# Value half of the up-projection from seven half-size products instead of eight

## The chip, the core and the metric

The kernel runs on one core of a Trainium2 chip. The metric is device time in microseconds (us) of one execution; lower is better. The core has a matrix engine (TensorE, "PE" in the profile; its weight loads are shown apart as "PEld"), three engines for elementwise work (VectorE "DVE", ScalarE "ACT", GpSimd "POOL") and a queue engine (SyncE "SP") that here issues nearly all transfers. Each engine runs its own instructions strictly in the order in which they are written; engines wait for one another only on semaphores. TensorE reads its operands from SBUF and adds up in the eight banks of PSUM (128 partitions x 512 float32 each).

## The reference

Two layers over x of shape (1, 512, 1024). Layer 0 mixes tokens by a Mamba-2 scan, layer 1 by causal pooling; each is followed by a gated feed-forward block, and that block is what the change touches:

```
def conv_ffn(u, w_up, conv_w, conv_b, w_down):
    h = u @ w_up                                  # (512,1024) x (1024,5632)
    h = causal_depthwise_conv(h, conv_w, conv_b)  # width 3, over tokens
    gate, val = split(h, 2)                       # 2816 columns each
    return (silu(gate) * val) @ w_down            # (512,2816) x (2816,1024)
```

All is float32, between RMS norms.

## The kernel before, in words

A float32 product is made of three passes on TensorE. Each operand is split in a high part (a copy rounded to TensorE's fp32r format) and a low part (the rest, by a subtraction), and `three_passes` (L306) adds high x high, high x low, low x high.

Weights come in slabs of 1 MB (128 partitions x 2048 numbers): in the up-projection a slab is 256 columns, so two output blocks of 128 columns, and eight k-blocks. SP loads slab n to `raw[n % 2]` (`load`, L263), which may be overwritten once slab n-2 has been split. ACT makes `w_hi` (`split_hi`, L268), DVE makes `w_lo` (`split_lo`, L274). There are two pairs of `w_hi`/`w_lo`, so a split also waits until TensorE has done with the slab two before.

The up-projection of a layer has 22 slabs, in 11 iterations of the index i: a slab of gate columns, then one of value columns (`up_pe`, L1142). A slab is 2 blocks x 8 k-blocks x 3 passes = 48 matmuls of 512 tokens, an iteration 96. The four blocks of an iteration are numbered q = 0 to 3 (0, 1 gate; 2, 3 value) and go to banks 4 to 7; `tmp` has one slot for each. After block q ACT makes the first tap of the convolution with the bias (`last_tap`, L524; the profile shows L525), DVE adds the other two (`other_taps`, L527; L534, each a 128x511 and a 128x510 instruction). After the gate blocks ACT makes the silu (L1171). DVE multiplies gate and value (L1189), ACT and DVE split the result to `act_hi` and `act_lo` (L1174, L1193), which the down-projection reads as its stationary operand.

The order of all this is written out by hand, one program for each engine. In an iteration ACT (`up_act`, L1152) runs: first taps q0 q1, silu q0 q1, split of the value slab, first taps q2 q3, `act_hi` twice; the split of the gate slab comes first. DVE (`up_dve`, L1177) runs: `split_lo`, taps q0 q1, `split_lo`, taps q2 q3, two products, two `act_lo`. Iterations 2 to 10 are a loop on the engine. The down-projection follows with 11 slabs of 48 matmuls (`down_pe`, L1040 in the profile).

GpSimd builds constants at the start, adds squares in the mixer (L862, a 128x512 addition) and does nothing in the feed-forward blocks.

## Time and profile before

| | |
|---|---|
| median of 3 runs | 1138.78 us (1138.66 to 1138.9) |
| profiled execution | 1138.84 us, of which span 1137.1 us |
| TensorE busy | 99% of the span |
| DVE, ACT, POOL busy | 61%, 46%, 3% |
| matmuls | 5730 |
| moved by DMA | 121.74 MB, mean 107 GB/s |

The profiled execution is one execution recorded by the hardware; its span runs from its first to its last recorded instruction. "Busy" is the share of the span in which an engine works on an instruction. TensorE's matmuls overlap in the records, so the distance between the starts of two of them, not the duration of one, says what a matmul costs.

### The profile page before, as it was taken

The numbers are of one execution on the slowest core, as the hardware profiler recorded it, in microseconds if no ns is written. First come the engines' busy times: TensorE is split into PE (matmuls) and PEld (weight loads), VectorE is DVE, ScalarE is ACT, GpSimd is POOL, SyncE is SP. The second block draws the span as 40 slices with busy tenths as digits, with TensorE's granted clock in tenths as the row PEclk, the third lists the DMA queues.
The fourth block names the chain that finished last, engine by engine and source line by source line (L and its number), as shares of the span: only waits on it lengthen the run. The fifth ranks groups of instructions, "written<-read, shape, count | busy, mean of one in ns | idle before, by whom it ended". The sixth has DMA issues, their size and how long they took to land.

```text
span 1137.1 us, 14741 instructions
## 1 busy us (share of the span) xinstructions
PE 1127.7 (99%) x5730; PEld 949.7 (84%) x5730; DVE 695.5 (61%) x825; ACT 524.2 (46%) x610; POOL 35.9 (3%) x93
## 2 busy tenths in 40 slices
PE   8999999999999999999999999999999999999998
PEld 7888888888888988888888888899888888888886
DVE  6778889999763865655655321597655565552124
ACT  5667676767533643443443221475443434331213
POOL 6000000000100000000000000000000000000000
PEclk9999999999999999999999999999999999999999
DMA  8244343433233133233233223512232232323221
GB/s 274 76 133 148 121 128 122 133 127 130 75 111 126 61 111 111 79 106 111 74 111 108 98 90 111 167 38 75 93 111 94 91 109 76 110 85 115 96 74 74
DMA packets 85390, 121.74 MB, mean 107 GB/s; under 512 B 4215, under 2 KB 71391, under 8 KB 85344
## 3 DMA queue, kind: packets, MB, share of 16 engines
q1 hardware_dynamic: 85162, 121.02, 32.0%
q8 instruction: 33, 0.54, 0.2%
q14 instruction: 13, 0.11, 0.0%
q10 hardware_dynamic: 182, 0.07, 0.0%
HBM read 118.92 MB, written 2.16 MB: 106 GB/s over the span
## 4 chain that ended last, share of the span: by engine, by line
PE 99%; DMA 1%; ACT 0%; DVE 0%; issue 0%; SPq 0%; DVEq 0%
PE bank L1040 29%; PE bank L307 19%; PE bank L308 19%; PE bank L309 19%; PE bank L515 6%; PE bank L801 1%; PE bank L792 1%; PE bank L753 1%; PE bank L743 1%; PE bank L431 1%; PE bank L1214 1%; DMA raw<-in_ssd_w_in 1%; PE bank L1229 0%; PE bank L1230 0%; PE bank L1231 0%; PE bank L721 0%
## 5 line engine op out<-in xcount | busy, mean ns | idle before, releaser
L307 PE MATMUL bank<-h_hi,w_hi 128*128 128x512 f32 x928 | 364.5, 393 | 0.0
L309 PE MATMUL bank<-h_hi,w_lo 128*128 128x512 f32 x928 | 361.5, 390 | 0.0
L308 PE MATMUL bank<-h_lo,w_hi 128*128 128x512 f32 x928 | 361.2, 389 | 0.0
L277 DVE TENSOR_TENSOR w_lo<-raw,w_hi 128x2048 fp32r<-128x2048 f32 x90 | 206.1, 2289 | 215.0 <-ACT w_hi L272 215.0
L534 DVE SCALAR_TENSOR_TENSOR tmp<-bank,par,tmp 128x511 f32<-128x511 f32 (+2 forms) x248 | 184.9, 747 | 125.3 <-ACT tmp L525 112.4
L272 ACT ACTIVATE w_hi<-raw 128x2048 fp32r<-128x2048 f32 x90 | 171.7, 1908 | 154.0 <-PE bank L1040 152.3
L309 PEld LDWEIGHTS bank<-h_hi,w_lo 128*128 128x128 f32 x928 | 174.2, 188 | 37.1
L307 PEld LDWEIGHTS bank<-h_hi,w_hi 128*128 128x128 f32 x928 | 174.3, 188 | 36.2 <-issue 0.8
L308 PEld LDWEIGHTS bank<-h_lo,w_hi 128*128 128x128 f32 x928 | 174.4, 188 | 35.0
L525 ACT ACTIVATE tmp<-bank,par 128x512 f32<-128x512 f32 x112 | 86.2, 774 | 221.7 <-PE bank L309 201.4
L1040 PE MATMUL bank<-w_lo,act_hi 128*128 128x512 f32 x348 | 107.2, 389 | 0.0
L1040 PE MATMUL bank<-w_hi,act_lo 128*128 128x512 f32 x348 | 107.1, 389 | 0.0
L1040 PE MATMUL bank<-w_hi,act_hi 128*128 128x512 f32 x348 | 107.1, 389 | 0.0
L1040 PEld LDWEIGHTS bank<-w_hi,act_lo 128*128 128x128 f32 x348 | 65.3, 188 | 13.6
L1040 PEld LDWEIGHTS bank<-w_lo,act_hi 128*128 128x128 f32 x348 | 65.3, 188 | 13.5
L1040 PEld LDWEIGHTS bank<-w_hi,act_hi 128*128 128x128 f32 x348 | 65.3, 188 | 13.4
L1174 ACT ACTIVATE act_hi<-tmp 128x512 f32 (+1 forms) x44 | 27.3, 633 | 55.8 <-DVE tmp L1189 55.8
L1040 PE MATMUL bank<-w_hi,y_hi 128*128 128x512 f32 x128 | 40.1, 394 | 0.0
L1171 ACT ACTIVATE tmp<-tmp 128x512 f32<-128x512 f32 x44 | 27.6, 626 | 26.5 <-DVE tmp L534 26.4
L1040 PE MATMUL bank<-w_lo,y_hi 128*128 128x512 f32 x128 | 39.5, 390 | 0.0
L1040 PE MATMUL bank<-w_hi,y_lo 128*128 128x512 f32 x128 | 39.5, 389 | 0.0
L1193 DVE TENSOR_TENSOR act_lo<-tmp,act_hi 128x512 f32 (+1 forms) x44 | 28.7, 690 | 6.3 <-ACT act_hi L1174 5.9
(203 smaller groups left out, 1030.1 us busy)
## 6 DMA issues: line engine op xcount, KB each, us to landing
raw<-in_ffn_w_up SPq DMA_DIRECT2D x44, 1024.0 KB, 5.0
raw<-in_ffn_w_down SPq DMA_DIRECT2D x22, 1024.0 KB, 4.8
raw<-in_ssd_w_in SPq DMA_DIRECT2D x19, 1024.0 KB, 5.2
decay<-ac_dram SPq DMA_DIRECT2D x16, 512.0 KB, 5.5
raw<-in_ssd_w_out SPq DMA_DIRECT2D x8, 1024.0 KB, 4.8
from_start<-ac_dram SPq DMA_DIRECT2D x32, 128.0 KB, 4.6
xres<-in_x SPq DMA_DIRECT2D x4, 512.0 KB, 6.0
result<-xres SPq DMA_DIRECT2D x3, 512.0 KB, 2.6
```

What stands on the lines that cost most here:

```text
L272: act.activation(w_parts(n, i)[0][:], raw[n % 2][:], ACT.Copy).then_inc(hi_ready, 1)
L277: dve.tensor_tensor(lo[:], raw[n % 2][:], hi[:].bitcast(F32), ALU.subtract).then_inc(lo_ready, 1)
L307: pe.matmul(dst, wh, xh, start=first, stop=False, **kw)
L308: pe.matmul(dst, wh, xl, start=False, stop=False, **kw)
L309: return pe.matmul(dst, wl, xh, start=False, stop=last, **kw)
L515: mm = pe.matmul(bank[:, 2 * s + j, ts], w[:, k, j * P:(j + 1) * P], x[:, k, ts], start=turn == 0 and k == 0, stop=turn == 2 and k == DB - 1)
L525: act.activation(tmp[:, slot, :], bank[:, source, :], ACT.Identity, bias=b, scale=w).then_inc(conv_tap, 1)
L534: dve.scalar_tensor_tensor(tmp[:, slot, back:], bank[:, source, 0:T - back], w, tmp[:, slot, back:], ALU.mult, ALU.add).then_inc(conv_part ...
L1040: mm = pe.matmul(bank[:, 2 * c + j, :], x[:, cs(c)], w[:, k, j * T:(j + 1) * T], start=start, stop=stop)
L1171: act.activation(tmp[:, j, :], tmp[:, j, :], ACT.Silu).then_inc(gate_silu, 1)
L1174: act.activation(act_hi[:, bass.ds(2 * i + j, 1), :].rearrange("p a l -> p (a l)"), tmp[:, 2 + j, :], ACT.Copy).then_inc(act_hi_ready, 1)
L1193: dve.tensor_tensor(act_lo[:, blk, :].rearrange("p a l -> p (a l)"), tmp[:, 2 + j, :], act_hi[:, blk, :].rearrange("p a l -> p (a l)").bit ...
```

## The change: seven products for the value slabs

In iterations 2 to 10 of each layer (18 value slabs in all; `SEVEN0 = 2`) the value slab is no longer 48 matmuls of 512 tokens. Weights (2 column blocks x 2 halves of k) and features (2 halves of k x 2 halves of the tokens) are taken as 2 x 2 blocks, and their product is made of seven block products instead of eight (Winograd's form of Strassen's scheme). A block product is 4 k-blocks x 3 passes = 12 matmuls of 256 tokens, so a slab is 84 of these (`seven_pe`), in banks 0 to 3.

What that adds:

- POOL forms the sums of feature blocks once per layer (`combos_pool`, ten 128x1024 instructions), ACT and DVE split them to `t_hi`, `t_lo` (four 128x1024 instructions each).
- POOL forms the four sums of weight blocks for each value slab in place, in `raw` (`weights_pool`, four instructions of 4x128 = 512 numbers per partition), after that slab has been split; ACT and DVE split the result, in two halves of 128x1024 (`weights_hi_act`, `weights_lo_dve`), to the other pair of `w_hi`/`w_lo`. `raw` is free only after that.
- ACT keeps the first product (`first_seven_act`, 128x256), and four DVE instructions add the seven up to the two value blocks in the SBUF tile `val` (`sevens_dve`). The taps of q2 and q3 read `val`.

What moves: the taps of q2 and q3 of an iteration and the split of the next value slab change places (the taps are ahead) on ACT and DVE. The product gate x value is kept unsplit in `gated`; `act_hi`/`act_lo` are gone, and their part is made in the down phase, one 128x1024 instruction on ACT and DVE for each down slab (`down_hi_act`, `down_lo_dve`; that of slab 0 in iteration 4). The loops are written out in full instead of looped. The first down slab begins with its chunks 2 and 3.

On DVE, in one iteration before (the loop's body from the value slab's split on; the pair of L534 rows stands twice, for q2 and q3):

```order
L277 TENSOR_TENSOR w_lo<-raw,w_hi 128x2048 [waits hi_ready]
...
L534 SCALAR_TENSOR_TENSOR tmp<-bank,par,tmp 128x511
...
L534 SCALAR_TENSOR_TENSOR tmp<-bank,par,tmp 128x510
...
L1189 TENSOR_TENSOR tmp<-tmp 128x512 [waits conv_done,gate_silu]
...
L1193 TENSOR_TENSOR act_lo<-tmp,act_hi 128x512
```

And an iteration on DVE after the change, from the second tap of q0 on (number 3; L1287 is `weights_lo_dve`, L1301 to L1308 are `sevens_dve`, the first L312 splits the next gate slab and the second the next value slab, L1381 is gate x value):

```order
L569 SCALAR_TENSOR_TENSOR tmp<-bank,par,tmp 128x510 [waits conv_part]
L1287 TENSOR_TENSOR w_lo<-raw,w_hi 128x1024 [waits ws_hi_ready] x2
L569 SCALAR_TENSOR_TENSOR tmp<-bank,par,tmp 128x511 [waits conv_tap]
L569 SCALAR_TENSOR_TENSOR tmp<-bank,par,tmp 128x510 [waits conv_part]
L312 TENSOR_TENSOR w_lo<-raw,w_hi 128x2048 [waits hi_ready]
L1301 TENSOR_TENSOR val<-val,bank 128x2x256 [waits p_done,p1_kept]
L1304 TENSOR_TENSOR val<-val,bank 128x2x256 [waits blk_done,c_step]
L1306 TENSOR_TENSOR val<-val,bank 128x256 [waits c_step]
L1308 TENSOR_TENSOR val<-val,bank 128x2x256 [waits c_step]
L569 SCALAR_TENSOR_TENSOR tmp<-val,par,tmp 128x511 [waits conv_tap]
...
L312 TENSOR_TENSOR w_lo<-raw,w_hi 128x2048 [waits hi_ready]
L1381 TENSOR_TENSOR gated<-tmp 128x512 [waits conv_done,gate_silu] x2
```

The taps of q2 and q3 now stand between the seven products' sums and the value slab's split, and both splits of a slab's sums stand between the taps of q0 and q1.

On ACT, the same iteration after the change (L1281 is `weights_hi_act`, L1339 the silu, L1294 the kept product):

```order
L560 ACTIVATE tmp<-val,par 128x512 [waits u_ready,c_ready] x2
L307 ACTIVATE w_hi<-raw 128x2048 [waits blk_done,slab_in1]
L560 ACTIVATE tmp<-bank,par 128x512 [waits u_ready,blk_done]
L1339 ACTIVATE tmp<-tmp 128x512 [waits conv_done]
L1281 ACTIVATE w_hi<-raw 128x1024 [waits w_sum,blk_done]
L1281 ACTIVATE w_hi<-raw 128x1024 [waits w_sum]
L560 ACTIVATE tmp<-bank,par 128x512 [waits u_ready,blk_done]
L1339 ACTIVATE tmp<-tmp 128x512 [waits conv_done]
L307 ACTIVATE w_hi<-raw 128x2048 [waits blk_done,slab_in0]
L1294 ACTIVATE val<-bank 128x256 [waits conv_done,blk_done]
```

The silu of q0 stands before the split of the sums, and the silu of q1 before the split of the next gate slab.

The diff, cut to its core:

```
         with ExitStack() as scope:
-            act_hi = sb("act_hi", [P, FB, T], F32R, scope=scope)
-            act_lo = sb("act_lo", [P, FB, T], F32R, scope=scope)
+            gated = sb("gated", [P, FB, T], scope=scope)
+            dn_hi0 = sb("dn_hi0", [P, 2, T], F32R, scope=scope)
+            t_hi = sb("t_hi", [P, 4, DB // 2, HALF], F32R, scope=scope)
...
+            dn_hi1 = sb("dn_hi1", [P, 2, T], F32R, scope=scope)
+            dn_lo0 = sb("dn_lo0", [P, 2, T], F32R, scope=scope)
+            with ExitStack() as values:
+                val = sb("val", [P, 2, 2, HALF], scope=values)
+            dn_lo1 = sb("dn_lo1", [P, 2, T], F32R, scope=scope)
+            dn_hi, dn_lo = [dn_hi0, dn_hi1], [dn_lo0, dn_lo1]
+        with ExitStack() as scope:
+            sb("gap_s", [P, 36 * KB], scope=scope)
...
+            if n >= 2 and seven_of(n - 2) is not None:
+                sp.wait_ge(ws_ready, 2 * seven_of(n - 2) + 2)
+            elif n >= 2:
+                sp.wait_ge(lo_ready, n - 1)
...
+            for c in (2, 3, 0, 1):
+                if c in banks_read:
+                    pe.wait_ge(*banks_read[c])
...
+        def seven_pe(pe, l, i):
+            n, t = S_UP[l] + 2 * i + 1, SEVENS * l + i - SEVEN0
+            own, other = w_slot(n), 1 - w_slot(n)
+            plain = lambda m, k: [quarter(w[own], m, k) for w in (w_hi, w_lo)]
+            summed = lambda m, k: [quarter(w[other], m, k) for w in (w_hi, w_lo)]
+            h = lambda k, half: [h_part(x, k, half) for x in (h_hi, h_lo)]
+            combo = lambda j: [x[:, j - 1, :, :] for x in (t_hi, t_lo)]
+            pe.wait_ge(lo_ready, n + 1)
+            if t:
+                pe.wait_ge(c_ready, t)
+            seven_product(pe, P1, plain(0, 0), h(0, 0))
+            seven_product(pe, P2, plain(0, 1), h(1, 0))
+            pe.wait_ge(t_ready7, 4 * (l + 1))
+            seven_product(pe, P4, plain(1, 1), combo(4)).then_inc(blk_done, 1)
+            pe.wait_ge(ws_ready, 2 * t + 1)
+            seven_product(pe, P7, summed(0, 0), combo(3))
+            seven_product(pe, P5, summed(1, 0), combo(1))
+            pe.wait_ge(ws_ready, 2 * t + 2)
+            seven_product(pe, P6, summed(1, 1), combo(2)).then_inc(p_done, 1)
+            seven_product(pe, P3, summed(0, 1), h(1, 1)).then_inc(blk_done, 1)
...
+            pool.wait_ge(h_ready, 8 * (1 + 2 * l) + 8)
+            step(t_sums(1), hi(0, 1), hi(0, 0), ALU.subtract)
+            step(t_sums(1), None, lo(0, 1), ALU.add)
+            step(t_sums(1), None, lo(0, 0), ALU.subtract, 4 * l + 1)
+            step(t_sums(2), hi(1, 1), view(t_sums(1)), ALU.subtract)
+            step(t_sums(2), None, lo(1, 1), ALU.add, 4 * l + 2)
+            step(t_sums(4), view(t_sums(2)), hi(1, 0), ALU.subtract)
+            step(t_sums(4), None, lo(1, 0), ALU.subtract, 4 * l + 3)
+            pool.wait_ge(t_ready7, 4 * l + 1)
+            step(t_sums(3), hi(1, 1), hi(0, 1), ALU.subtract)
+            step(t_sums(3), None, lo(1, 1), ALU.add)
+            step(t_sums(3), None, lo(0, 1), ALU.subtract, 4 * l + 4)
...
+        def combo_view(tile, j):
+            return tile[:, j - 1, :, :].rearrange("p k n -> p (k n)")
+
+        def combos_hi_act(act, l, turns):
+            for c in turns:
+                j = T_ORDER[c]
+                act.wait_ge(t_sum, 4 * l + c + 1)
+                act.activation(combo_view(t_hi, j), t_sums(j), ACT.Copy).then_inc(t_hi_ready, 1)
+
+        def combos_lo_dve(dve, l, turns):
+            for c in turns:
+                j = T_ORDER[c]
+                dve.wait_ge(t_hi_ready, 4 * l + c + 1)
+                dve.tensor_tensor(combo_view(t_lo, j), t_sums(j), combo_view(t_hi, j).bitcast(F32),
+                                  ALU.subtract).then_inc(t_ready7, 1)
+
+        def weights_pool(pool, l, i):
+            n, t = S_UP[l] + 2 * i + 1, SEVENS * l + i - SEVEN0
+            a11, a21, a12, a22 = (quarter(raw[n % 2], m, k) for k in range(2) for m in range(2))
...
+        def weights_pool(pool, l, i):
+            n, t = S_UP[l] + 2 * i + 1, SEVENS * l + i - SEVEN0
+            a11, a21, a12, a22 = (quarter(raw[n % 2], m, k) for k in range(2) for m in range(2))
+            pool.wait_ge(lo_ready, n + 1)
+            pool.tensor_tensor(a11, a11, a21, ALU.subtract).then_inc(w_step, 1)
+            pool.wait_ge(w_step, 2 * t + 1)
+            pool.tensor_tensor(a21, a21, a22, ALU.add).then_inc(w_sum, 1)
+            pool.wait_ge(w_sum, 2 * t + 1)
+            pool.tensor_tensor(a22, a22, a11, ALU.subtract).then_inc(w_step, 1)
+            pool.wait_ge(w_step, 2 * t + 2)
+            pool.tensor_tensor(a12, a12, a22, ALU.subtract).then_inc(w_sum, 1)
+
+        def weights_hi_act(act, l, i):
+            n, t = S_UP[l] + 2 * i + 1, SEVENS * l + i - SEVEN0
+            act.wait_ge(blk_done, CB + 2 * FB * l + 4 * i + 2)
+            for j, part in enumerate((FIRST_PART, LAST_PART)):
+                act.wait_ge(w_sum, 2 * t + j + 1)
+                act.activation(w_hi[1 - w_slot(n)][:, part], raw[n % 2][:, part], ACT.Copy).then_inc(ws_hi_ready, 1)
+
+        def weights_lo_dve(dve, l, i):
+            n, t = S_UP[l] + 2 * i + 1, SEVENS * l + i - SEVEN0
+            for j, part in enumerate((FIRST_PART, LAST_PART)):
+                dve.wait_ge(ws_hi_ready, 2 * t + j + 1)
+                dve.tensor_tensor(w_lo[1 - w_slot(n)][:, part], raw[n % 2][:, part],
+                                  w_hi[1 - w_slot(n)][:, part].bitcast(F32), ALU.subtract).then_inc(ws_ready, 1)
+
+        def first_seven_act(act, l, i):
+            act.wait_ge(blk_done, CB + 2 * FB * l + 4 * i + 3)
+            if i > SEVEN0:
+                act.wait_ge(conv_done, CONV0[l] + 4 * i)
+            act.activation(val[:, 0, 1, :], seven_half(P1), ACT.Copy).then_inc(p1_kept, 1)
+
+        def sevens_dve(dve, l, i):
+            t = SEVENS * l + i - SEVEN0
+            both = lambda ap: ap.unsqueeze(1).to_broadcast([P, 2, HALF])
+            dve.wait_ge(p1_kept, t + 1)
+            dve.wait_ge(p_done, t + 1)
+            dve.tensor_tensor(val[:, :, 0, :], both(val[:, 0, 1, :]), seven_pair(P2), ALU.add).then_inc(c_step, 1)
+            dve.wait_ge(c_step, 3 * t + 1)
+            dve.wait_ge(blk_done, CB + 2 * FB * l + 4 * i + 4)
+            dve.tensor_tensor(val[:, :, 1, :], both(val[:, 1, 0, :]), seven_pair(P5), ALU.add).then_inc(c_step, 1)
+            dve.wait_ge(c_step, 3 * t + 2)
+            dve.tensor_tensor(val[:, 1, 0, :], val[:, 1, 1, :], seven_half(P4), ALU.subtract).then_inc(c_step, 1)
+            dve.wait_ge(c_step, 3 * t + 3)
+            dve.tensor_tensor(val[:, :, 1, :], val[:, :, 1, :], seven_pair(P3), ALU.add).then_inc(c_ready, 1)
+
+        def up_source(i, q):
+            if i >= SEVEN0 and q >= 2:
+                return val[:, q - 2, :, :].rearrange("p a n -> p (a n)")
+            return bank[:, q if i == 0 else 4 + q, :]
...
         def up_pe(pe, l, i):
-            for s in range(2):
+            for s in range(2 if i < SEVEN0 else 1):
                 pe.wait_ge(lo_ready, S_UP[l] + s + 1 + 2 * i)
                 for j in range(2):
                     q = 2 * s + j
-                    if not isinstance(i, int) or i > 1:
+                    if i > 1:
                         pe.wait_ge(conv_done, CONV0[l] + q - 3 + 4 * i)
-                    block_product(pe, bank[:, 4 + q, :], (S_UP[l] + s) % 2, j).then_inc(blk_done, 1)
-
+                    block_product(pe, bank[:, 4 + q, :], w_slot(S_UP[l] + s + 2 * i), j).then_inc(blk_done, 1)
+            if i >= SEVEN0:
+                seven_pe(pe, l, i)
+
+        def up_tap_act(act, l, i, q):
+            s, j = q // 2, q % 2
+            if s == 1 and i >= SEVEN0:
+                act.wait_ge(c_ready, SEVENS * l + i - SEVEN0 + 1)
+            else:
+                act.wait_ge(blk_done, CB + 2 * FB * l + q + 1 + 4 * i)
+            act.wait_ge(u_ready, 1 + FB * l + 2 * i)
+            blk = s * FB + j + 2 * i
+            last_tap(act, q, up_source(i, q), col("ffn_w", (l * FFN_TAPS + FFN_TAPS - 1) * 2 * FB + blk),
+                     col("ffn_b", l * 2 * FB + blk))
+
...
+            if i > SEVEN0:
                 for j in range(2):
-                    q, blk = 2 * s + j, s * FB + j
-                    act.wait_ge(blk_done, CB + 2 * FB * l + q + 1 + 4 * i)
-                    if s == 0:
-                        act.wait_ge(u_ready, 1 + FB * l + 2 * i)
-                    else:
-                        act.wait_ge(act_ready, 1 + FB * l + 2 * i)
-                    last_tap(act, q, up_bank(i, q), col("ffn_w", (l * FFN_TAPS + FFN_TAPS - 1) * 2 * FB + blk + 2 * i),
-                             col("ffn_b", l * 2 * FB + blk + 2 * i))
-                if s == 0:
+                    up_tap_act(act, l, i - 1, 2 + j)
+            split_hi(act, n + 1, (blk_done, base))
+            up_tap_act(act, l, i, 0)
+            up_silu_act(act, l, i, 0)
+            if i == SEVEN0 + 2:
+                down_hi_act(act, l, 0)
+            weights_hi_act(act, l, i)
+            up_tap_act(act, l, i, 1)
+            up_silu_act(act, l, i, 1)
+            split_hi(act, n + 2, (blk_done, base + 3))
+            first_seven_act(act, l, i)
+            if i == UP_SLABS // 2 - 1:
+                for j in range(2):
+                    up_tap_act(act, l, i, 2 + j)
...
+            up_taps_dve(dve, l, i, 0)
+            if i == SEVEN0 + 2:
+                down_lo_dve(dve, l, 0)
+            weights_lo_dve(dve, l, i)
+            up_taps_dve(dve, l, i, 1)
+            split_lo(dve, n + 2)
+            sevens_dve(dve, l, i)
             for j in range(2):
-                act.wait_ge(u_ready, 1 + FB * l + j + 1 + 2 * i)
-                act.activation(act_hi[:, bass.ds(2 * i + j, 1), :].rearrange("p a l -> p (a l)"),
-                               tmp[:, 2 + j, :], ACT.Copy).then_inc(act_hi_ready, 1)
-
...
+                up_taps_dve(dve, l, i, 2 + j)
+            if i < UP_SLABS // 2 - 1:
+                split_lo(dve, n + 3)
             for j in range(2):
-                dve.wait_ge(gate_silu, FB * l + j + 1 + 2 * i)
-                dve.wait_ge(conv_done, CONV0[l] + 2 + j + 1 + 4 * i)
...
+        def down_hi_act(act, l, s):
+            act.wait_ge(u_ready, 1 + FB * l + 2 * s + 2)
+            if s == 1:
+                act.wait_ge(blk_done, CB + 2 * FB * (l + 1))
+            if s >= 2:
+                act.wait_ge(rows_used, 6 + 9 * l + s - 1)
+            act.activation(dn_hi[s % 2][:, :, :], gated[:, 2 * s:2 * s + 2, :], ACT.Copy).then_inc(dn_hi_ready, 1)
+
+        def down_lo_dve(dve, l, s):
+            dve.wait_ge(dn_hi_ready, DOWN_SLABS * l + s + 1)
+            dve.tensor_tensor(dn_lo[s % 2][:, :, :], gated[:, 2 * s:2 * s + 2, :], dn_hi[s % 2][:, :, :].bitcast(F32),
+                              ALU.subtract).then_inc(dn_ready, 1)
 
...
+            combos_pool(pool, 0)
+            for i in range(SEVEN0, UP_SLABS // 2):
+                weights_pool(pool, 0, i)
             pool.wait_ge(tr_done, 8 * 2 + 2)
             pool.tensor_copy(win_main[:, :, 0:EDGE], win_edge[:, :, :]).then_inc(win_ready, 1)
+            combos_pool(pool, 1)
+            for i in range(SEVEN0, UP_SLABS // 2):
+                weights_pool(pool, 1, i)
 
...
+            for i in range(2, UP_SLABS // 2):
                 up_dve(dve, 0, i)
             for s in range(1, DOWN_SLABS - 1):
+                down_lo_dve(dve, 0, s)
                 split_lo(dve, S_DOWN[0] + s)
+            down_lo_dve(dve, 0, DOWN_SLABS - 1)
             pool_weights_dve(dve)
```

## Rows read from the trace of the kernel before

**Rows 1.** The page, parts 1 and 4: engines' busy time, and the last chain.

```profile
PE 1127.7 (99%) x5730; PEld 949.7 (84%) x5730; DVE 695.5 (61%) x825; ACT 524.2 (46%) x610; POOL 35.9 (3%) x93
PE 99%; DMA 1%; ACT 0%; DVE 0%; issue 0%; SPq 0%; DVEq 0%
```

**Rows 2.** Timeline of PE: start, duration (us), line, operation; 96 matmuls apart.

```profile
439.75 0.39 PE L308 MATMUL bank<-h_lo,w_hi 128*128 128x512 f32 x1
...
461.51 0.39 PE L308 MATMUL bank<-h_lo,w_hi 128*128 128x512 f32 x1
```

**Rows 3.** The same view, matmuls of 256 tokens in the first up slabs.

```profile
384.26 2.06 PE L515 MATMUL bank<-h_lo,wf_hi 128*128 128x256 f32 x16
386.15 2.06 PE L515 MATMUL bank<-h_hi,wf_lo 128*128 128x256 f32 x16
388.05 0.71 PE L431 MATMUL bank<-ident,stage 128*128 128x128 f32 x5
```

**Rows 4.** Timeline of DVE over one iteration; the bracket is the wait before.

```profile
832.33 2.29 DVE L277 TENSOR_TENSOR w_lo<-raw,w_hi 128x2048 fp32r<-128x2048 f32 x1 [2.50 <-ACT w_hi L272]
...
839.05 1.64 DVE L534 SCALAR_TENSOR_TENSOR tmp<-bank,par,tmp 128x511 f32<-128x511 f32 x2 [2.88 <-ACT tmp L525]
840.61 1.28 DVE L1189 TENSOR_TENSOR tmp<-tmp 128x512 f32<-128x512 f32 x2
...
844.52 2.29 DVE L277 TENSOR_TENSOR w_lo<-raw,w_hi 128x2048 fp32r<-128x2048 f32 x1 [0.97 <-ACT w_hi L272]
846.73 0.74 DVE L534 SCALAR_TENSOR_TENSOR tmp<-bank,par,tmp 128x511 f32<-128x511 f32 x1
847.62 0.75 DVE L534 SCALAR_TENSOR_TENSOR tmp<-bank,par,tmp 128x510 f32<-128x510 f32 x1 [0.15 <-DVE tmp L534]
849.94 1.64 DVE L534 SCALAR_TENSOR_TENSOR tmp<-bank,par,tmp 128x511 f32<-128x511 f32 x2 [1.57 <-ACT tmp L525]
854.08 2.29 DVE L277 TENSOR_TENSOR w_lo<-raw,w_hi 128x2048 fp32r<-128x2048 f32 x1 [2.50 <-ACT w_hi L272]
```

**Rows 5.** Timeline of ACT in the same iteration.

```profile
849.01 0.78 ACT L525 ACTIVATE tmp<-bank,par 128x512 f32<-128x512 f32 x1 [3.87 <-PE bank L309]
...
851.61 0.63 ACT L1171 ACTIVATE tmp<-tmp 128x512 f32<-128x512 f32 x1 [1.30 <-DVE tmp L534]
852.15 1.90 ACT L272 ACTIVATE w_hi<-raw 128x2048 fp32r<-128x2048 f32 x1
```

**Rows 6.** Groups by form: count, busy us, mean ns of one, idle before.

```profile
L862 POOL TENSOR_TENSOR sq_sum<-sq_sum,sq 128x512 f32<-128x512 f32 x12 | 17.1, 1428 | 260.2 <-ACT sq L856 260.2
...
L927 DVE TENSOR_TENSOR xdt<-bank,dt 128x512 f32<-128x512 f32 x16 | 11.0, 688 | 8.0 <-PE bank L743 7.8
...
L989 DVE TENSOR_TENSOR y_lo<-xbc,y_hi 128x1024 fp32r<-128x1024 f32 x8 | 10.6, 1322 | 29.0 <-ACT y_hi L876 28.9
...
L961 DVE TENSOR_TENSOR tmp<-bank,from_start 128x384 f32<-128x384 f32 x16 | 8.8, 550 | 8.6 <-PE bank L792 8.6
...
L303 DVE TENSOR_TENSOR w_lo<-raw,w_hi 128x1024 fp32r<-128x1024 f32 x1 | 1.3, 1304 | 0.1
L297 DVE TENSOR_TENSOR w_lo<-raw,w_hi 128x1024 fp32r<-128x1024 f32 x1 | 1.2, 1207 | 0.0
...
L289 ACT ACTIVATE w_hi<-raw 128x1024 fp32r<-128x1024 f32 x1 | 1.1, 1057 | 0.2 <-DMA raw<-in_ssd_w_in 0.2
```

**Rows 7.** Timeline of POOL in the mixer.

```profile
290.90 1.29 POOL L862 TENSOR_TENSOR sq_sum<-sq_sum,sq 128x512 f32<-128x512 f32 x1 [10.77 <-ACT sq L856]
298.13 2.60 POOL L862 TENSOR_TENSOR sq_sum<-sq_sum,sq 128x512 f32<-128x512 f32 x1 [5.94 <-ACT sq L856]
```

**Rows 8.** Timeline of DVE at the same two moments.

```profile
291.21 2.06 DVE L989 TENSOR_TENSOR y_lo<-xbc,y_hi 128x1024 fp32r<-128x1024 f32 x1
...
297.30 2.28 DVE L277 TENSOR_TENSOR w_lo<-raw,w_hi 128x2048 fp32r<-128x2048 f32 x1
```

**Rows 9.** The page, part 6: transfers, KB each, median us from issue to landing.

```profile
raw<-in_ffn_w_up SPq DMA_DIRECT2D x44, 1024.0 KB, 5.0
```

**Rows 10.** A stretch's row: us, busy (instructions) per engine, granted clock, DMA.

```profile
1130.00:1137.10 7.10, 1.71 (x8) 1.09 (x6) 3.39 (x6) 1.96 (x6) 0.00 (x0) 0.85 0.38 148
```

220 lines of the change are left out of this document (141 added, 79 removed).

## The prediction

> **What bounds the kernel now.** I read the page first: TensorE is busy 99% of the span, and 99% of the chain that ended last is TensorE [rows 1]. The reader is to see that nothing else sets the time: DVE has 61%, ACT 46%. Then the timeline of PE: 96 matmuls of 512 tokens start in 21.76 us, 0.227 us each [rows 2], so an iteration of the up-projection (96 matmuls) takes 21.76 us, and DVE repeats itself at just that distance (832.33 and 854.08) [rows 4]. The profiled execution took 1138.84 us, its span and 1.7 us around it; that is within 0.1 us of the median 1138.78, so I add to 1138.8.
>
> But DVE and ACT are not idle because they have little to do in this stretch. Of an iteration's 21.76 us DVE waits only about 8, in waits that all name ACT (2.50, 2.88, 0.97, 1.57) [rows 4]; ACT in turn waits for DVE or for a block of TensorE [rows 5]. So the question is whether the two, with what the change gives them, can still follow.
>
> **What TensorE saves.** A value slab is 84 matmuls of 256 tokens instead of 48 of 512. Matmuls of 256 with a new weight each start 16 in 1.89 us and 16 in 1.90 [rows 3], 0.1185 us each, more than half of 0.227. The slab is 84 x 0.1185 = 9.95 us instead of 10.88. The saving is 0.93 us a slab, 16.7 us for 18. If TensorE stays the bound, an iteration is 20.83 us.
>
> **What DVE and ACT get, step by step.** Both run in order, and both orders are in the listings of the change. I follow the one loop that goes through them, from the end of the low split of value slab i on DVE (time 0) to the end of that of slab i+1. Each step waits for the one before, or stands behind it on its engine:
>
> - gate x value, two of 128x512, 1.28 us [rows 4]: 1.28
> - first tap of q0 on ACT; it waits for both products, since it overwrites what they read (`tmp`). 0.78, and DVE starts 0.15 later [rows 4, 5]: 2.21
> - taps of q0 on DVE, 1.64 [rows 4]: 3.85
> - silu q0 on ACT, 0.63 [rows 5]: 4.48
> - first half of the high part of the weight sums, 1.06 [rows 6]: 5.54
> - the two halves of their low part, 1.30 and 1.21 [rows 6]: 8.05
> - taps of q1, 1.64: 9.69
> - silu q1, 0.63, and behind it the high split of the next gate slab, 1.90 [rows 5]: 12.22
> - its low split, 2.29 [rows 4]: 14.51. Only now may TensorE begin the next iteration.
> - the seven products' sums: three instructions of 512 numbers with a PSUM input at 0.69, one of 256 at about 0.42 (128x384 takes 0.55), and three waits for the one before at 0.15 [rows 4, 6]: 2.94, so 17.45
> - first tap of q2 on ACT, 0.93 with the handover: 18.38
> - taps of q2 and q3, 3.28: 21.66
> - low split of value slab i+1, 2.29: 23.95. Its high part (after the tap of q3 on ACT, 0.7 + 1.9 us beside 3.28 of DVE) is ready in time.
>
> An instruction that was already queued starts up to 0.09 us before the end shown of the one ahead (844.52 + 2.29 against 846.73) [rows 4]; six such places take off 0.5. The loop is then 23.4 us. That is above 21.76 and above TensorE's 20.83: TensorE would wait for the gate slab, which it never did.
>
> **What GpSimd adds.** The four weight sums follow the value slab's low split. An addition of 512 numbers took 1.29 us [rows 7]; strided operands as here are not in the trace. Four, with 0.07 allowed between them, are 5.4 us. The ACT step that needs the second pair comes at 5.54 + 0.1, so by themselves they just fit. But they meet DVE. At 298.13 such an addition took 2.60, exactly as long as the DVE split that had begun at 297.30 still ran (to 299.58), plus its own time [rows 7, 8]; at 291.21 a DVE subtraction of 1024 numbers took 2.06 beside an addition that ran to 292.19, where the group's other seven average (10.6 - 2.06)/7 = 1.22 [rows 6 to 8]. One waits for the other for the whole instruction. So one GpSimd addition comes into the loop: either between the two products, or in front of the first low half of the sums: +1.3 us. The loop is 24.7.
>
> The Trainium skill (SBUF — State Buffer, "Who interferes with whom") says which instructions this hits: a DVE instruction with two SBUF inputs against a GpSimd one that reads SBUF, while one with at most one SBUF input is spared. The two pairs of rows agree. By it the taps of q0 and q1, which read PSUM, run beside the additions, as I count them.
>
> Bounds. From below: the two never meet in the loop, 23.4. From above: each addition takes the longest that the trace has, 2.60. Then the second pair is ready about 5.2 us later, and the loop is near 29 to 30. I take 1.3: the twelve additions of the trace average 1.43, and without the one of 2.60 (17.1 - 2.6)/11 = 1.32 [rows 6, 7]. Part of the way to the upper bound is kept in the range (rival B).
>
> **The ends.** The loop governs iterations 3 to 10: eight intervals of 24.7, 197.6. Iteration 4 has the split of down slab 0 besides, 1.25. The first interval (start of iteration 2 to start of 3): ACT makes the first tap of q3, two splits of feature sums of 128x1024 (1.06 each) and the high split, 4.9 us; DVE has taps, products, two low halves of 1.3 and its split, about 8.7 at the end; then 14.5 - 0.3 + 1.3 of the loop: 24.2. The ten feature sums of GpSimd have no row; by their size 2 x 1.3 each, the last three can start only after the first `t_lo` in iteration 1, which puts them 1 to 4 us late. I take 26. At the end the second down slab needs 2.9 + 0.9 + 3.3 + 1.3 + 1.3 + 2.3 - 0.4 = 11.6 us after the first began, TensorE's 48 matmuls take 10.9: 0.7 more. After that a down slab costs DVE 1.3 + 2.3 and ACT 1.1 + 1.9 in 10.88 us: hidden. The removed `act_hi`/`act_lo` give nothing by themselves beyond being out of the loop, which the sum already has.
>
> A layer's nine iterations: 26 + 197.6 + 1.25 + 0.7 = 225.6 us against 9 x 21.76 = 195.8: +29.8. Two layers: +59.6. **Forecast: 1138.8 + 59.6 = 1198.4 us.**
>
> Costed at nothing: loads. A value slab's buffer is free only after the second low half, 8 us into the loop, plus 5.0 for the load [rows 9], 13; its split comes after 18. The gate's has a whole period. The longer instruction streams: without the loops' register instructions they should be no slower; unknown, small.
>
> **Rivals.**
>
> A, the loop without the collision: 23.4. Intervals 24.7 + 187.2 + 1.25 + 0.7 = 213.9, +18.1 a layer: 1175. For it: the collision needs both at the same moment, and an addition may slip into one of ACT's steps. Against: GpSimd is released by the very split in front of the products.
>
> B, slow additions: strided and in place, 1.8 us each, between 1.3 and 2.6. Now they set the pace: the fourth ends near 0.64 + 4 x 1.87 = 8.1, the second high half (1.06) and low half (1.21) at 10.4, where 8.05 + 1.3 = 9.35 stood. With handovers of 0.1 that is 1.3 later: the loop is 26.0, the first interval 27.5. 27.5 + 208 + 1.25 + 0.7 = 237.5, +41.7 a layer: 1222. For it: no strided row. Against: the additions of the same size at 1.3.
>
> C, the other side: TensorE stays the bound and the change gives what it saves, 1138.8 - 16.7 = 1122. It decides at a loop of 20.83 for the full gain, and of 21.76 for any. For it: busy time of DVE in the loop is only 17.9 by my list (1.28 + 4 x 1.64 + 2.51 + 2 x 2.29 + 2.94 = 17.9), so all depends on the waits for ACT, about 6 us: two first taps, two silus, a half split and a whole one. Against: each of these waits is written into the order, and 1.6 us of them would have to vanish even without the collision.
>
> D, the clock. TensorE will now stand still in each iteration: about 4 us of 24.7. In the trace the granted clock is at its full level in all stretches but the last, 0.85 of full, in which TensorE worked 1.7 of 7.1 us [rows 10]. Short drops are covered by the same 4 us. If it stayed at the lower level, half, for the whole stretch, an iteration would be 2 x 20.83 = 41.7 us: 1138.8 + 18 x 19.9 = 1497. The Trainium skill (TensorE: Matmul & The Clock Gate, Part 1) says that the clock halves after an idle stretch and comes back after sustained work; the trace agrees for the end of the kernel, and nothing in it shows stops as short as these.
>
> **How the numbers follow.** Forecast 0.55 (own range 1186 to 1212: 0.7 us either way on the loop), A 0.18, B 0.16, C 0.07, D 0.04. The range leaves out C, D and the far part of B: 1168 to 1232. Measured changes within 0.2% (2.3 us) are none that this kernel can tell. Faster by more: 0.07 (C). Within: 0.02, a loop of 21.7. Slower: 0.91.
>
> **What would show it.** Right: TensorE starts gate blocks 24 to 25.5 us apart, and waits each time for the low split of the gate slab; the wait inside the value slab, before the fourth product, is shorter; DVE near 75% busy in the stretch, waiting for ACT; in each iteration one product, or one low half of the sums, or one addition is long by about 1.3. If the sums' additions are 1.8 each, it is B; if no instruction is stretched, A; if TensorE's matmuls follow one another through a whole iteration, C, and my loop is wrong in its waits, most likely in the silu steps that I let stand in front of the splits. A granted clock below full in the middle of the kernel would speak for D. The down phase should look as before but for its second slab.

## The result, and the profile after

The changed kernel takes 1180.17 us (median of 4 runs, 1180.1 to 1180.33), the kernel before 1138.84 in the same session: a ratio of 1.0362 (1.0344 to 1.038), slower by 41.3 us. I had forecast 1198.4 with a range of 1168 to 1232. Direction and range hold; the size is 18 us off, and outside the 1186 to 1212 that I had given the likeliest case alone. Rival A's 1175 lies nearer to the measured time than the forecast does; whether its mechanism does too is asked below.

The page of the changed kernel, parts 1 and 4, answers to [rows 1]:

```profile
PE 1129.7 (96%) x6378; PEld 973.9 (83%) x6378; DVE 820.2 (70%) x919; ACT 566.0 (48%) x650; POOL 202.9 (17%) x185
PE 67%; DVE 19%; issue 7%; ACT 5%; POOL 1%; DMA 0%; DVEq 0%; ACTq 0%; SPq 0%; POOLq 0%
```

The chain that ended last was 99% TensorE; now a third of it is DVE, ACT and the gaps between them. Yet by the distances of its matmuls TensorE did get less to do. Its timeline shows a value slab's matmuls of 256 tokens (start, duration, line; 19 more lie between the two rows):

```profile
897.84 0.28 PE L342 MATMUL bank<-h_hi,w_hi 128*128 128x256 f32 x1
...
900.23 0.28 PE L344 MATMUL bank<-h_hi,w_lo 128*128 128x256 f32 x1
```

Twenty steps in 2.39 us are 0.120 each (predicted 0.1185 from [rows 3]); the slab's 84 take 10.07 us and a gate slab's 48 of 512 take 10.91. So TensorE needs 20.98 us for an iteration. It gets 23.55, as DVE's timeline over one iteration shows (start, duration, line, operation, count, and in brackets the wait before; it answers to [rows 4]):

```profile
909.16 2.29 DVE L312 TENSOR_TENSOR w_lo<-raw,w_hi 128x2048 fp32r<-128x2048 f32 x1 [2.50 <-ACT w_hi L307]
911.38 0.68 DVE L1301 TENSOR_TENSOR val<-val,bank 128x512 f32<-128x512 f32 x1
...
914.84 2.98 DVE L569 SCALAR_TENSOR_TENSOR tmp<-val,par,tmp 128x511 f32<-128x511 f32 x4 [0.89 <-ACT tmp L560]
917.74 2.28 DVE L312 TENSOR_TENSOR w_lo<-raw,w_hi 128x2048 fp32r<-128x2048 f32 x1
919.94 2.38 DVE L1381 TENSOR_TENSOR gated<-tmp 128x512 f32<-128x512 f32 x2
923.23 1.53 DVE L569 SCALAR_TENSOR_TENSOR tmp<-bank,par,tmp 128x511 f32<-128x511 f32 x2 [0.91 <-ACT tmp L560]
926.41 2.36 DVE L1287 TENSOR_TENSOR w_lo<-raw,w_hi 128x1024 fp32r<-128x1024 f32 x2 [1.65 <-ACT w_hi L1281]
928.68 1.53 DVE L569 SCALAR_TENSOR_TENSOR tmp<-bank,par,tmp 128x511 f32<-128x511 f32 x2
932.71 2.29 DVE L312 TENSOR_TENSOR w_lo<-raw,w_hi 128x2048 fp32r<-128x2048 f32 x1 [2.50 <-ACT w_hi L307]
```

The gate slab's low split stands at 909.16 and at 932.71: a round of 23.55 us (the prediction had named 24 to 25.5 as the sign of its loop). All waits of DVE name ACT. ACT's timeline in the same round, against [rows 5], closes the ring, as I call the loop through both engines:

```profile
922.41 0.78 ACT L560 ACTIVATE tmp<-bank,par 128x512 f32<-128x512 f32 x1 [5.10 <-DVE gated L1381]
924.79 0.63 ACT L1339 ACTIVATE tmp<-tmp 128x512 f32<-128x512 f32 x1 [1.60 <-DVE tmp L569]
925.33 1.99 ACT L1281 ACTIVATE w_hi<-raw 128x1024 fp32r<-128x1024 f32 x2
...
930.25 0.63 ACT L1339 ACTIVATE tmp<-tmp 128x512 f32<-128x512 f32 x1 [2.26 <-DVE tmp L569]
930.78 1.90 ACT L307 ACTIVATE w_hi<-raw 128x2048 fp32r<-128x2048 f32 x1
```

ACT's first tap (922.41) waited 5.10 us for DVE's products, its silu (924.79) for the taps, the high halves of the sums (925.33) stand behind that silu, the second silu (930.25) waits for the second taps, and the gate slab's high split (930.78) stands behind it. Neither engine is full (in 906.9 to 930.5 DVE is busy 17.4 us, ACT 10.1); they wait in turn.

GpSimd's timeline shows the four weight sums, which had no row before:

```profile
920.10 1.67 POOL L1268 TENSOR_TENSOR raw<-raw 128x512 f32<-128x512 f32 x1 [18.56 <-DVE w_lo L312]
921.85 1.62 POOL L1270 TENSOR_TENSOR raw<-raw 128x512 f32<-128x512 f32 x1
923.55 1.30 POOL L1272 TENSOR_TENSOR raw<-raw 128x512 f32<-128x512 f32 x1
924.93 1.30 POOL L1274 TENSOR_TENSOR raw<-raw 128x512 f32<-128x512 f32 x1
```

Strided and in place an addition costs 1.30, as the unstrided ones of [rows 7]. The first two are longer because they meet the products, and the products (2.38 for two, 1.28 in [rows 4]) because they meet them. The taps of q0 at 923.23 read PSUM, lie beside the third addition, and neither is stretched.

TensorE's waits over the whole execution (what it waited for, us in total, times, longest):

```profile
PE bank L342 <- DVE w_lo L312: 22.7, 15, 3.1
PE bank L342 <- DVE w_lo L1287: 12.9, 18, 1.8
PE bank L1075 <- DVE w_lo L312: 4.2, 3, 1.4
```

Once a round it waits for the gate slab's low split, once for the low halves of the sums; in a usual round these waits are 1.36 and 0.70 us. The prediction had named both, and the second as the shorter. The longest, 3.1, stands once a layer, at the start of iteration 3.

### The profile page after: what moved, and what is told of

Same layout as the page of the kernel before. It is cut to its first block, busy times and chain, and to the rows that moved or that the text cites. A ratio compares the mean times of both kernels' runs of the same rounds, so it can differ in the third digit from the quotient of the medians.

```text
span 1178.5 us, 15389 instructions
## 1 busy us (share of the span) xinstructions
PE 1129.7 (96%) x6378; PEld 973.9 (83%) x6378; DVE 820.2 (70%) x919; ACT 566.0 (48%) x650; POOL 202.9 (17%) x185
## 3 DMA queue, kind: packets, MB, share of 16 engines
HBM read 118.92 MB, written 2.16 MB: 103 GB/s over the span
## 4 chain that ended last, share of the span: by engine, by line
PE 67%; DVE 19%; issue 7%; ACT 5%; POOL 1%; DMA 0%; DVEq 0%; ACTq 0%; SPq 0%; POOLq 0%
PE bank L1075 27%; PE bank L342 9%; PE bank L344 9%; PE bank L343 9%; DVE tmp L569 7%; PE bank L550 6%; DVE gated L1381 3%; DVE w_lo L312 3%; ACT tmp L560 2%; DVE w_lo L1287 2%; PE bank L836 1%; ACT w_hi L1281 1%; ACT w_hi L307 1%; PE bank L788 1%; PE bank L827 1%
## 5 line engine op out<-in xcount | busy, mean ns | idle before, releaser
L342 PE MATMUL bank<-h_hi,w_hi 128*128 128x512 f32 (+1 forms) x856 | 317.2, 371 | 22.9 <-DVE w_lo L312 22.7
L344 PE MATMUL bank<-h_hi,w_lo 128*128 128x512 f32 (+1 forms) x856 | 311.9, 364 | 0.0
L343 PE MATMUL bank<-h_lo,w_hi 128*128 128x512 f32 (+1 forms) x856 | 311.7, 364 | 0.0
L312 DVE TENSOR_TENSOR w_lo<-raw,w_hi 128x2048 fp32r<-128x2048 f32 x90 | 210.9, 2343 | 60.8 <-ACT w_hi L307 60.8
L569 DVE SCALAR_TENSOR_TENSOR tmp<-bank,par,tmp 128x511 f32<-128x511 f32 (+1 forms) x176 | 130.6, 747 | 40.5 <-ACT tmp L560 36.9
L1075 PE MATMUL bank<-w_hi,dn_hi 128*128 128x512 f32 x348 | 107.7, 391 | 4.2 <-DVE w_lo L312 4.2
L1075 PE MATMUL bank<-w_lo,dn_hi 128*128 128x512 f32 x348 | 107.2, 389 | 0.0
L1075 PE MATMUL bank<-w_hi,dn_lo 128*128 128x512 f32 x348 | 107.1, 389 | 0.0
L342 PE MATMUL bank<-t_hi,w_hi 128*128 128x256 f32 x288 | 84.0, 292 | 12.9 <-DVE w_lo L1287 12.9
L343 PE MATMUL bank<-t_lo,w_hi 128*128 128x256 f32 x288 | 82.1, 285 | 0.0
L344 PE MATMUL bank<-t_hi,w_lo 128*128 128x256 f32 x288 | 82.0, 285 | 0.0
```

Of the source, the lines that this page charges most:

```text
L312: dve.tensor_tensor(lo[:], raw[n % 2][:], hi[:].bitcast(F32), ALU.subtract).then_inc(lo_ready, 1)
L342: pe.matmul(dst, wh, xh, start=first, stop=False, **kw)
L343: pe.matmul(dst, wh, xl, start=False, stop=False, **kw)
L344: return pe.matmul(dst, wl, xh, start=False, stop=last, **kw)
L569: dve.scalar_tensor_tensor(tmp[:, slot, back:], source[:, 0:T - back], w, tmp[:, slot, back:], ALU.mult, ALU.add).then_inc(conv_part if j ...
L1075: mm = pe.matmul(bank[:, 2 * c + j, :], x[:, cs(c)], w[:, k, j * T:(j + 1) * T], start=start, stop=stop)
```

## The experiments

The name "round" below is the distance between two gate splits on DVE, 23.55 us in the changed kernel. Each kernel was compared with the kernel before, whose median was 1138.7 to 1138.8 in all of these.

**The collision of GpSimd with the products.** The edit, in the changed kernel's `weights_pool`; this kernel leaves most of each sum out, and only its time is of use:

```
-            a11, a21, a12, a22 = (quarter(raw[n % 2], m, k) for k in range(2) for m in range(2))
+            a11, a21, a12, a22 = (quarter(raw[n % 2], m, k)[:, 0:1, 0:8] for k in range(2) for m in range(2))
```

> The changed kernel, but GpSimd forms the four weight sums over 8 of their 512 numbers only, so that most of each sum is left out and GpSimd holds nothing for long in the loop. The order, the waits and all else stay. Theory (a loop through DVE and ACT sets the pace, 23.55 us, of which 1.09 is one GpSimd addition that DVE has to wait out): the pair of products falls from 2.38 to 1.29 us and the loop to 22.45; eight intervals a layer, so 16 x 1.1 and about 2 x 1 to 2 in the two first intervals: 1180 - 20 = 1160 us (1157 to 1163). Rival (GpSimd only fills time in which DVE would wait anyway): 1180. Rival (the slower clock at the start of each gate slab sets the pace): 1180.

Measured: 1156.38 us (1156.08 to 1156.69), ratio 1.0155 (1.0126 to 1.0185): 23.8 us less than the changed kernel. DVE's timeline:

```profile
913.93 2.29 DVE L312 TENSOR_TENSOR w_lo<-raw,w_hi 128x2048 fp32r<-128x2048 f32 x1 [2.50 <-ACT w_hi L307]
...
924.71 0.68 DVE L1381 TENSOR_TENSOR gated<-tmp 128x512 f32<-128x512 f32 x1
```

A product takes its 0.68 again, two of them 1.29; the round is 22.46 (891.47 to 913.93), 1.09 shorter, which is what the pair of products had grown by (2.38 less 1.29). Shown: the collision costs 1.09 us a round, 17.4 us in 16 rounds. The rest is nearly all in the first interval: on DVE the gate split of iteration 3 follows the value split before it after 11.67 us (436.80 to 448.47) instead of 15.00 (436.91 to 451.91), 3.3 a layer.

**The silu in front of the gate split.** In `up_act`:

```
-            up_silu_act(act, l, i, 1)
             split_hi(act, n + 2, (blk_done, base + 3))
+            up_silu_act(act, l, i, 1)
```

> One instruction moved on ACT: the high split of the next gate slab stands ahead of the silu of q1, which has to wait for DVE's taps of q1. Theory (the 2.50 us for which DVE waits before the gate slab's low split are in the loop): DVE finds the high part ready after its taps of q1, the loop goes from 23.55 to about 21.2 to 21.7, 16 times about 2.1 less: 1145 us (1141 to 1151). Rival (TensorE's own sequence is the pace, the split only waits for it): no change, 1180. If the loop were gone altogether, TensorE's 20.96 a round would give 1180 - 16 x 2.6 = 1139.

Measured: 1146.45 us (1146.3 to 1146.5), ratio 1.0068 (1.0045 to 1.0091), and a round of 21.72. DVE's timeline shows the gate split without its wait of 2.50, and a new wait, for a product of TensorE. TensorE's own waits are below it:

```profile
907.23 2.28 DVE L312 TENSOR_TENSOR w_lo<-raw,w_hi 128x2048 fp32r<-128x2048 f32 x1
...
910.92 0.69 DVE L1304 TENSOR_TENSOR val<-val,bank 128x512 f32<-128x512 f32 x1 [0.75 <-PE bank L344]
```
```profile
PE bank L342 <- DVE w_lo L1287: 11.4, 19, 1.6
```

One line moved gives back 33.7 of the 41.3 us. The ring now goes through TensorE: it waits for the first low half of the sums (0.49 us at 904.79), and DVE waits for the last of the seven products behind that.

**The taps ahead of the value split, undone.** This is the second half of the change's own description. On both engines:

```
 # ACT
+            split_hi(act, n + 1, (blk_done, base))
             if i > SEVEN0:
                 for j in range(2):
                     up_tap_act(act, l, i - 1, 2 + j)
-            split_hi(act, n + 1, (blk_done, base))
 # DVE
+            if i < UP_SLABS // 2 - 1:
+                split_lo(dve, n + 3)
             for j in range(2):
                 up_taps_dve(dve, l, i, 2 + j)
-            if i < UP_SLABS // 2 - 1:
-                split_lo(dve, n + 3)
```

> The changed kernel with one part undone: the split of the next value slab stands ahead of the taps of q2 and q3 on ACT and on DVE, the rest stays. Theory: GpSimd's additions then begin while DVE has the four taps of val (two SBUF inputs) and the products before it, so more than one of them is waited out; the loop gets longer, to about 25.3, 16 x 1.8: 1208 us (1190 to 1215). Rival (the weight sums come earlier, and they are what everything waits for): shorter than 1180, 1165 to 1175.

Measured: 1210.76 us (1210.67 to 1210.84), ratio 1.0633 (1.0602 to 1.0664), round 25.43 (953.98 to 979.41). So the order "taps ahead" is worth 30.6 us within the change. DVE and GpSimd, the two timelines apart:

```profile
906.69 2.28 DVE L312 TENSOR_TENSOR w_lo<-raw,w_hi 128x2048 fp32r<-128x2048 f32 x1
908.90 5.84 DVE L569 SCALAR_TENSOR_TENSOR tmp<-val,par,tmp 128x511 f32<-128x511 f32 x4
914.66 2.38 DVE L1381 TENSOR_TENSOR gated<-tmp 128x512 f32<-128x512 f32 x2
```
```profile
909.06 1.73 POOL L1268 TENSOR_TENSOR raw<-raw 128x512 f32<-128x512 f32 x1 [18.61 <-DVE w_lo L312]
...
914.27 1.62 POOL L1274 TENSOR_TENSOR raw<-raw 128x512 f32<-128x512 f32 x1
```

GpSimd is released at 908.9 and now meets, besides the products (2.38 as before), the four taps that read `val` and `tmp`, both in SBUF: 5.84 us instead of 2.98. Against that +2.86 stands the wait of 0.89 for ACT's tap, which the split now fills: +1.97, and the round grew by 1.88. The collision does not vanish when the split goes first; it spreads to more DVE instructions.

**The kernel before, its loops written out.** Six `with engine.Fori(2, UP_SLABS // 2) as i:` became `for i in range(...)`.

> The kernel before with the loops of TensorE, ACT and DVE written out in full, nothing else. For the error of my sum: theory (the 0.15 us between the two taps of a block, and the 0.1 us at handovers, belong to the looped code, where a separate instruction waits and registers are counted): the pair of taps takes 1.53 us instead of 1.64 in the up-projection, DVE's waits shrink, and the time stays at 1138.8 since TensorE is the bound. Rival (they belong to the dependence itself): 1.64 stays. Time within 0.1% in both.

Measured: 1138.66 us, ratio 0.9999 (0.9988 to 1.0011). DVE's timeline:

```profile
833.73 1.53 DVE L534 SCALAR_TENSOR_TENSOR tmp<-bank,par,tmp 128x511 f32<-128x511 f32 x2
```

The time is the same, TensorE being the bound, but the pair of taps takes 1.53 where it took 1.64 in the loop [rows 4]. Writing the loops out costs nothing by itself (in the changed kernel, where DVE and ACT set the pace, the loops were not put back), and it is the cause of one error of mine (below).

**The first half of the sums ahead of the first silu as well.** On top of the moved silu, ACT runs tap q0, first high half, silu q0, tap q1, second high half, gate split, silu q1; DVE puts the first low half ahead of the taps of q1 (and, in iteration 4, the split of down slab 0 behind the second low half):

```
+            weights_hi_act(act, l, i, [0])
             up_silu_act(act, l, i, 0)
 ...
             up_tap_act(act, l, i, 1)
-            weights_hi_act(act, l, i)
+            weights_hi_act(act, l, i, [1])
 # DVE
+            weights_lo_dve(dve, l, i, [0])
+            up_taps_dve(dve, l, i, 1)
+            weights_lo_dve(dve, l, i, [1])
-            weights_lo_dve(dve, l, i)
-            up_taps_dve(dve, l, i, 1)
```

> On top of e2 (the gate slab's high split ahead of the silu): the first high half of the weight sums stands ahead of the silu of q0, and the taps of q1 between the two low halves, on ACT and DVE. e2's loop of 21.72 us goes through TensorE: DVE waits 0.75 for the seventh product, TensorE 0.6 for the low halves of the sums. Theory (what binds is now the way from the value slab's split over the products, which hold GpSimd up, to the second low half, and these stand where they stood): nearly no change, 21.7, 1145 to 1147 us. Rival (each wait removed on DVE counts): 1 us a round less, 1130.

Measured: 1131.19 us, ratio 0.9933 (0.9913 to 0.9953); and again, with more rounds:

> The kernel of e3_order_only again, for its interval: 1131.2 us, 0.66% below the kernel before, with every theory.

1131.22 us (1131.09 to 1131.62), ratio 0.9935 (0.9921 to 0.9948). My theory had said that nearly nothing more would come; it fell. DVE's timeline and TensorE's waits:

```profile
912.15 1.26 DVE L1291 TENSOR_TENSOR w_lo<-raw,w_hi 128x1024 fp32r<-128x1024 f32 x1
913.60 1.53 DVE L569 SCALAR_TENSOR_TENSOR tmp<-bank,par,tmp 128x511 f32<-128x511 f32 x2 [0.19 <-ACT tmp L560]
915.75 1.23 DVE L1291 TENSOR_TENSOR w_lo<-raw,w_hi 128x1024 fp32r<-128x1024 f32 x1 [0.61 <-ACT w_hi L1284]
```
```profile
PE bank L342 <- DVE w_lo L1291: 1.0, 3, 0.4
...
PE bank L342 <- DVE w_lo L312: 0.4, 2, 0.2
```

The first low half now begins 1.45 us after the taps before it (910.70, 912.15), where 3.18 lay between them (900.33, 903.51 with the moved silu alone). That half was what TensorE waited for. The second half, which I had taken for the limit, comes no later than it is needed. TensorE runs through: in the later iterations it starts gate blocks 20.98 us apart (DVE's rounds are 20.92 there, since DVE catches up after iteration 4). This version beats both kernels, 7.5 us or 0.65% below the one before. That the two steps belong together, the run with one of them alone shows further down.

**The floor.** The moved silu together with the additions over 8 numbers; again most of each sum is left out.

> e2 with GpSimd's four weight sums over 8 of their 512 numbers (most of each sum left out). Both theories of where the saving went are asked at once: with neither the wait for ACT nor GpSimd in the loop, TensorE should run through. Theory (the seven products save what the matmuls' distances say: 48 x 0.227 + 84 x 0.120 = 20.96 a round against 21.76): 16 x 0.76 less than e2 and 2 to 3 for the first rounds: 1131 to 1134 us, so under the kernel before by about 0.5%. Rival (the small matmuls cost more than their distance, or the slower clock does): at or above 1138.

Measured: 1129.62 us (1129.42 to 1129.77), ratio 0.992 (0.9903 to 0.9936), round 20.98 (893.74 to 914.72 on DVE). So TensorE's saving exists, 21.76 less 20.98, 0.78 a slab; the version with the whole sums and the better order lies 1.6 us above this.

**More slots.** On top of the better order two more slots of `tmp`, so that the first tap need not wait for the products, which then run after the taps of q1 of the next iteration, outside the additions; the down split of slab 0 goes to the last iteration. On ACT the silu of q1 also goes behind the kept product. The core of the edit:

```
+                tmp2 = sb("tmp2", [P, 2, T], scope=second)
+        def up_slot(i, q):
+            return q + 4 if q < 2 and i > SEVEN0 and i % 2 == 1 else q
 # DVE, i > SEVEN0, between the two low halves
+                for j in range(2):
+                    up_mul_dve(dve, l, i - 1, j)
```

> e3, whole computation, with two more slots for the gate blocks of every second iteration, so that the product gate x value of iteration i-1 can stand after the taps of q1 of iteration i; the split of the first down slab's input moves from iteration 4 to 10. Theory (the pair of products, which ACT's first tap and GpSimd's sums wait behind, is taken out of the loop): TensorE is the bound again, 20.96 a round, 1134 us (1131 to 1137), below the kernel before. Rival (the collisions with GpSimd just move to other DVE instructions): 21.5 or more, 1142 to 1147.

Measured: 1131.18 us (1131.14 to 1131.24), ratio 0.9933 (0.9917 to 0.995): the same as without the slots. The DVE busy time falls from 821.6 to 802.5 us: two products take 1.28 again. One collision is left, the fourth addition, which begins 0.19 us behind the first low half (910.71) and takes 2.18 instead of 1.30:

```profile
910.90 2.18 POOL L1279 TENSOR_TENSOR raw<-raw 128x512 f32<-128x512 f32 x1
```

So the collision with the products is gone, and that buys nothing, since TensorE already ran through: once the order is right, the stretched products cost no time.

**The pool weights behind the last down split.** On top of that, two lines swapped at the end of layer 0:

```
-            pool_weights_dve(dve)
 ...
+            pool_weights_dve(dve)
```

> e8, and in layer 0 the scaling of the pool mixer's weights (one DVE instruction of 2.3 us) stands behind the low split of the last down slab instead of ahead of it. Theory (the down phase of layer 0 got 1.8 us longer since the low part of gate x value now stands in that DVE stretch ahead of the last split): 1.8 us less than e8, 1132. Rival (the 1.8 us come from another place of that phase): same as e8.

Measured: 1132.76 us (1132.08 to 1133.45), ratio 0.9949 (0.9932 to 0.9966): not 1.8 less than without the swap, but 0.9 to 2.3 more. TensorE's waits, first without the swap and then with it:

```profile
PE bank L1080 <- DVE w_lo L314: 2.0, 3, 1.4
```
```profile
PE bank L1459 <- DVE stage L444: 1.9, 1, 1.9
...
PE bank L1080 <- DVE w_lo L314: 0.5, 2, 0.3
```

The wait for the last down split falls from 2.0 to 0.5, and a wait of 1.9 for DVE's norm appears 12 us later (736.19, where the other stood at 724.44): the scaling of the pool weights has only changed what it delays. This profile is of the run of 1132.08; why two of the four runs took 1.3 us more is open.

**The half alone.** Of the edits that made the better order only one, the first high half ahead of the first silu, on top of the changed kernel; DVE as in the changed kernel.

```
+            weights_hi_act(act, l, i, [0])
             up_silu_act(act, l, i, 0)
 ...
-            weights_hi_act(act, l, i)
+            weights_hi_act(act, l, i, [1])
```

> The changed kernel with the other step of e3 alone: the first high half of the weight sums ahead of the silu of q0 on ACT (DVE's order unchanged). Theory (steps of a loop are not added up; GpSimd's fourth addition ends at 926.2 in the changed kernel's round, 0.9 us after ACT now wants the second half): the first low half starts 1.6 us earlier, but the second stays where GpSimd puts it, and the loop falls by only 0.2 to 0.3: 16 x 0.25, 1176 us (1174 to 1178). Rival (the wait of 1.65 us ahead of the low halves goes altogether): 16 x 1.6, 1154.

Measured: 1184.33 us (1184.02 to 1184.64), ratio 1.0401 (1.0382 to 1.042): 4.2 us more than the changed kernel, where I had expected a gain. DVE's timeline, then GpSimd's, of a long round:

```profile
927.36 1.25 DVE L1291 TENSOR_TENSOR w_lo<-raw,w_hi 128x1024 fp32r<-128x1024 f32 x1
930.94 1.23 DVE L1291 TENSOR_TENSOR w_lo<-raw,w_hi 128x1024 fp32r<-128x1024 f32 x1 [2.33 <-ACT w_hi L1284]
...
936.11 2.29 DVE L312 TENSOR_TENSOR w_lo<-raw,w_hi 128x2048 fp32r<-128x2048 f32 x1 [2.50 <-ACT w_hi L307]
```
```profile
927.61 2.15 POOL L1274 TENSOR_TENSOR raw<-raw 128x512 f32<-128x512 f32 x1
```

The first low half is early, as wanted (927.36). But it has two SBUF inputs and begins just ahead of GpSimd's fourth addition, which takes 2.15 instead of 1.30; the second high half waits for that addition, the second low half 2.33 for it, and the taps of q1, silu and gate split stand behind. In layer 1 rounds alternate between 24.3 (911.85 to 936.11) and 23.4 (936.11 to 959.52); in a short one the addition is 1.29. In the better order the fourth addition takes 2.15 too (912.41), but there the taps of q1 stand in the gap. The same step that helps when the silu has moved and DVE fills the gap costs time by itself.

What makes a round short is TensorE. TensorE's first matmul of the short round, and ACT's first high half in it:

```profile
938.46 0.80 PE L342 MATMUL bank<-h_hi,w_hi 128*128 128x512 f32 x1 [3.02 <-DVE w_lo L312]
```
```profile
951.21 1.06 ACT L1284 ACTIVATE w_hi<-raw 128x1024 fp32r<-128x1024 f32 x1 [1.06 <-PE bank L344]
```

After the long round TensorE has waited 3.02 us, and its next matmuls (939.05 to 941.61) start 0.43 us apart instead of 0.227, the lower level of its clock. So the gate blocks end late, the first high half waits 1.06 for them and not for GpSimd, the first low half starts at 952.30, and the addition (951.87) is ahead of it. The trace has seven rounds in which the first high half waits for TensorE, and in all seven TensorE's clock had fallen at the start of the round; those rounds take 23.4 us, one 23.9. In the others but iteration 4 the addition takes 2.15 or 2.16. This is read from one trace; no run sets the clock apart from the rest.

## Why the prediction was right, and where it was off

**TensorE's saving** was right: 0.1185 a matmul predicted, 0.120 measured; an iteration of 20.98 instead of 20.83, 0.15 us.

**The loop through DVE and ACT** was right as a mechanism: the steps are in the trace in the order given, and moving one of them (the silu) took the round from 23.55 to 21.72. Its size was off: 24.7 predicted, 23.55 measured. Step by step, from start to start, in the round of the rows above:

| step | predicted | measured |
|---|---|---|
| products, to the first tap, collision included | 2.58 | 2.47 |
| tap to taps of q0, to silu | 0.93 + 1.64 | 0.82 + 1.56 |
| silu, first high half, to low half | 0.63 + 1.06 | 0.54 + 1.08 |
| two low halves | 2.51 | 2.27 |
| taps of q1, silu | 1.64 + 0.63 | 1.57 + 0.53 |
| gate split, high and low | 1.90 + 2.29 | 1.93 + 2.21 |
| sums of the products, to the tap of q2 | 2.94 | 2.60 |
| tap, four taps | 0.93 + 3.28 | 0.86 + 2.90 |
| value split, low | 2.29 | 2.20 |
| sum | 25.25, less 0.5 | 23.54 |

No step is off by more than 0.4, and nearly all are off to the same side. The term that I mis-sized is the handover between instructions. I had taken 0.15 for one that waits for the one ahead on its own engine, from the pair of taps in [rows 4], and 0.5 in all for overlaps of queued instructions. But [rows 4] come from inside an engine loop, and the changed kernel's code is written out: there the pair takes 1.53, and so it does in the kernel before with its loops written out. The step of the sums is 0.34 us shorter than I had it and the eight tap instructions 0.52 (1.64 to 1.53 twice, 3.28 to 2.98), together 0.86 of the 1.2 us; the collision is 0.2 smaller; the rest is overlap, which occurs at most handovers and not at six. The trace of before had the taps in unrolled code too (in the mixer, at 250.58, three instructions of L534 take 2.31 us, 0.77 each, where the pair has 0.82), and I should have taken the durations there. What in the looped code makes the difference is not settled by these runs.

**The collision** was right: 1.3 predicted, 1.09 measured, at the products, the first of the three places that I had named. I had counted the taps reading PSUM as spared, and they are (923.23, 1.53 us beside an addition). The taps that read `val` are not: 5.84 for 2.98 when the order is undone. The Trainium skill (SBUF — State Buffer, "Who interferes with whom") says that a DVE instruction with two SBUF inputs contends with a GpSimd instruction that reads SBUF and that issue order decides who blocks; both rows agree, and the half alone shows the other side of it, GpSimd blocked (2.15 for 1.30). One reading in the prediction is too exact: 2.60 is not the 1.45 us that the split still ran plus 1.29, which is 2.74, but 0.14 less.

**The sum over a layer.** From the start of iteration 2 to the first down slab the predicted 225.6 us stand against 214.95 and 214.92 measured (428.89 to 643.84 and 837.90 to 1052.82 by TensorE's first matmuls): 25.4 instead of 26 for the first interval, 189.6 instead of 198.85 for the other eight with the down split, and nothing instead of 0.7 for the second down slab. That is 21.3 us too much in two layers. Against it stand terms that I left out, about 3 us: in iteration 1 TensorE lost 0.44 us in layer 0 and 0.66 in layer 1, behind products and splits that met GpSimd's feature sums; 1.8 at the end of layer 0, where DVE has the scaling of the pool weights ahead of the last split; 0.4 at the kernel's end, less 0.15 at its start. 1198.4 - 21.3 + 3 is 1180.1. All these terms are measured, so their sum shows only that none is missing; and the forecast's error would have been 21 us had the omissions not worked against it.

The first of these, on DVE's timeline, where a pair of products and a split that take 1.28 and 2.28 alone take 5.21 and 4.01; GpSimd's additions of 1024 numbers beside them are in the second fence:

```profile
410.12 5.21 DVE L1381 TENSOR_TENSOR gated<-tmp 128x512 f32<-128x512 f32 x2
...
424.82 4.01 DVE L312 TENSOR_TENSOR w_lo<-raw,w_hi 128x2048 fp32r<-128x2048 f32 x1 [0.40 <-ACT w_hi L307]
```
```profile
409.58 2.40 POOL L1221 TENSOR_TENSOR t_new<-t_new,h_hi 128x1024 f32<-128x1024 f32 x1
412.06 2.72 POOL L1221 TENSOR_TENSOR t_new<-t_new,h_lo 128x1024 f32<-128x1024 f32 x1
```

**The rivals.** A (no collision, 1175) is nearer in number, 5 us where the forecast is 18 off, and wrong in mechanism: the round of 23.55, near its 23.4, has a collision of 1.09 in it and shorter handovers. That A comes nearer is luck. B (additions of 1.8) did not occur, they take 1.30. C (TensorE stays the bound) did not occur. The prediction had named the place where its loop would have to be wrong for C, "most likely in the silu steps that I let stand in front of the splits", and these steps are what holds TensorE up: with both moved, and DVE's first low half ahead of the taps of q1, the bound is TensorE again. The 1131.2 us of that order are not C's 1122: TensorE's round is 0.15 longer than I had it (2.7 us in 18), layer 0's up-projection takes 212.8 us (iterations 1 to 10, 406.8 to 619.6 by TensorE's matmuls) where 217.6 less 9 x 0.78 would be 210.6, so 2.2 a layer are lost in iterations 1, 2 and 4, and the 1.8 at the end of layer 0 stays.

D (the clock) did not occur as a lasting state, but left a trace. One such place on TensorE's timeline, right after a wait of 3.10 us, stands in the first fence (start, duration); the second has a row for each of two iterations, with its length, each engine's busy time and instructions, the granted clock, the DMA share and GB/s:

```profile
454.26 0.80 PE L342 MATMUL bank<-h_hi,w_hi 128*128 128x512 f32 x1 [3.10 <-DVE w_lo L312]
454.85 0.63 PE L343 MATMUL bank<-h_lo,w_hi 128*128 128x512 f32 x1
455.28 0.63 PE L344 MATMUL bank<-h_hi,w_lo 128*128 128x512 f32 x1
```
```profile
430.73:454.26 23.53, 19.90 (x127) 17.70 (x125) 16.09 (x15) 9.65 (x10) 8.80 (x6) 1.00 0.24 83
454.26:477.80 23.54, 22.77 (x132) 20.25 (x132) 17.35 (x19) 10.01 (x11) 5.89 (x4) 0.93 0.27 90
```

In the second row the granted clock is 0.93 on average: from 454.85 on six distances are 0.43 us instead of 0.227, so at the lower of the two levels (1.2 GHz), and then the full one returns. That is about 1.4 us, inside the iteration's slack, so it cost nothing: both rounds are 23.5. It happened three times: after both waits of 3.10 us (454.26 and 863.28) and once inside a value slab, after a wait of 1.83 (904.14); that slab ended late, and TensorE's wait for the next gate split shrank to nearly nothing. This was in iteration 4, which took 24.69 us, and 24.70 in layer 0 without the lower clock.

## What to carry to other kernels

When engines run their own orders and hand work to each other, write the ring of waits down step by step, from start to start, before looking at busy shares: here DVE at 70% and ACT at 48% set the time, and one ACT instruction in front of another was worth 33.7 of 41.3 us. Take the durations from code of the same form (written out or looped), and subtract the overlap at every handover. A GpSimd addition beside DVE's taps from PSUM stretched neither; beside the products, with two SBUF operands, four additions cost 1.09 us a round (of an addition's 1.30), beside the products and the taps of `val`, which they stretched by 2.86, the round grew by 1.88 more; and once TensorE was the bound, the stretched products cost nothing. An edit in a ring can help or harm by what other edits stand with it, so try the pair as well as the single one.

## What was unexpected of the hardware

- The same two dependent tap instructions take 1.64 us in an engine loop and 1.53 written out, with no difference in the kernel's time while TensorE is the bound.
- GpSimd's addition of 512 float32 numbers in each partition takes 1.30 us, contiguous ([rows 7]) or in four blocks of 128 (the weight sums), and one of 1024 takes 2.40, in place or not; beside DVE with two SBUF inputs 1.62 to 2.18 and 2.72 to 4.37.
- In the changed kernel the lower clock followed both of TensorE's waits of 3.10 us, one of the two of 1.83 and 1.84 (904.14, not 495.14), and none of the waits of 1.36. With the half alone (1184.33 us) it followed the wait of 3.02 at 598.91 and not the one of 3.03 at 574.65. With that kernel and with the value split first (1210.76) it was seen more often, and the mean granted clock of the profiled executions was 0.986 and 0.981. What decides it is open.
- With the half alone the lower clock made rounds shorter, 23.4 us instead of 24.3: a late TensorE held back the DVE instruction that would otherwise have blocked GpSimd.
